# Moving four weight loads ahead of SyncE's wait for the scattered rows

## Chip, cores, metric

The kernel runs on one core of a Trainium2 chip. The metric is the time of one execution in microseconds of device time, as the median of several runs. The engines are named TensorE (PE in the profile, PEld for its weight loads), VectorE (DVE), ScalarE (ACT), GpSimd (POOL) and SyncE (SP). SyncE, ScalarE and GpSimd each have a queue on which they issue DMAs. All these DMAs are carried out by the core's 16 DMA engines.

## What is computed

One layer of a mixer with attention, spatial gating and a recurrence, then a mixture of experts over 512 tokens of width 1024. Only the second part matters here (16 experts of width 512, two for each token):

```python
def hierarchical_moe(x, wg, bg, we, be, w_gate, w_up, w_down):
    ...
    expert_id = g_idx[:, None] * EXPERTS_PER_GROUP + top_i
    combine = jnp.sum(jax.nn.one_hot(expert_id, N_EXPERTS, dtype=jnp.float32)
                      * (g_w * top_p)[..., None], axis=1).astype(x.dtype)
    y = jnp.zeros_like(xt)
    for e in range(N_EXPERTS):
        h = jax.nn.silu(xt @ w_gate[e]) * (xt @ w_up[e])
        y = y + combine[:, e:e + 1] * (h @ w_down[e])
    return y.reshape(b, s, d)
```

## The kernel before

The kernel doesn't run every expert over every token. It computes the router's choice for four blocks of 128 tokens (t = 0 to 3), gives each token and each of its two experts a place (`slot_idx`), and scatters the normalised rows `xn2` into the DRAM tensor `slots`, grouped by expert and padded to tiles of 128 rows. `scatter(t)` on GpSimd (line 640) issues two indirect DMAs for each block of tokens, so eight in all, 512 KB each; each raises the semaphore `scattered` by 16. Then the experts' tiles run one after the other. A tile is 128 rows of one expert.

Each matmul in f32 is made of three, with operands split in a high and a low part. So each 512 KB block of weights that lands is first copied to `w_hi` by ScalarE (L371, L378), then VectorE subtracts it to give `w_lo` (L383, L389), then TensorE uses both (`expert_block`, L1352; its matmuls are L1052 to L1054). `w_hi` and `w_lo` have four slots, so a split waits until TensorE has used the block four before it.

A tile has twelve blocks: r = 0 to 3 of the gate weights, r = 4 to 7 of the up weights, and r = 8 to 11 of the down weights. **The down blocks that stand in a tile belong to the tile before it**, because a tile's hidden values are ready only when its gate and up products are. The blocks land alternately in two sets of twelve buffers, `EVEN` and `ODD` (lines 307 to 311), each with a semaphore of its own (`even_in`, `odd_in`). The second tile uses `ODD`; its r = 8 to 11 are `raw_mg` buffers 3 to 6 and hold the down weights of expert 0.

A tile's rows are read from `slots` by SyncE (`load_rows`, L503), into `x_odd` or `x_even`, then turned by eight transposes on TensorE (`turn_x`, L1342), copied as high part by ScalarE (L922) and as low part by VectorE (L1958). The first tile is an exception: its rows are gathered by matmuls (`place0`, L1295), not read. So the first rows that go through `slots` are those of the second tile, and TensorE turns them between blocks 5 and 6 of the first tile (L1372, L1373). Later tiles' rows are turned ahead of block 8 of the tile before. The results of a tile are stored back to `slots` by ScalarE (L943, and L1028 for the one before the last) and gathered by GpSimd at the end (L656).

SyncE works through its program in order; whatever stands behind a wait of its own is issued later. Around the change its program is: first tile's gate and up blocks (`EVEN`, L492), second tile's gate and up blocks (`ODD`, L498; its last three, into `raw_mg`, wait until TensorE is done with the output projection's weights), then the wait for all eight scatters (L525), the read of the second tile's rows (L526), the four down blocks (L528), the read of the third tile's rows (L530), then the third tile's blocks. `load_rows` also waits for the semaphore `xT_ps`, which TensorE raises in the first tile behind its block 0 (L1371). Each of the loads is one DMA of 512 KB.

Of the kernel before, what the change touches and what calls it, by code (L numbers as in the profile page):

```python
# [32 lines left out]
NT = TOK // P  # L33
# [61 lines left out]
PER_EXPERT = TOK // P  # L95
# [18 lines left out]
def build(nc, a, out):  # L114
# [10 lines left out]
    with ctx:  # L125
        def sem(name):
            return ctx.enter_context(nc.semaphore(name))
# [146 lines left out]
        def y_hi(t):  # L274
# [6 lines left out]
        S = {n: sem(n) for n in (  # L281
            "g1_spread ones_done x0_sq_done x0_stat x0_rstd x0_norm x0_turned xn_hi_done xn_done "
            "hi_act lo_pool lo_dve w_used taken "
            "ident_done consts_pool consts_dve zero_done zeros_stored "
            "g1_in chan_in diag_in sgu_in relb_in toep_filled toep_out bias_in bias_done route_in g2_in "
            "sgu_raw sguT_ps sguT_done mask_done sv_sq sv_stat sv_rstd sv_done sp_exp chan_done "
            "conv_done gates_ps gates_done "
            "decay_done mult_in mult_done u_done c_mid b_mid ch bh c_ready b_ready mix_ps "
            "scores_ps biased exped normed probsT_ps probsT_done out_ps a_hi a_ready "
# [40 lines left out]
        x_even, x_odd, y_even, y_odd = (xn2[:, n, :] for n in range(4))  # L330
# [77 lines left out]
        def _(sp):  # L408
# [10 lines left out]
            def load_block(places, r, src):  # L419
                bufs, sems = places  # L420
                sp.dma_start(bufs[r].rearrange("p (k n) -> p k n", k=2), src).then_inc(sems[r], 16)

            def tile_source(e, before, r):

                if r < 4:
                    return rows2(w_g[e], 2 * r, 0)
                if r < 8:
                    return rows2(w_u[e], 2 * (r - 4), 0)
                return rows2(w_d[before], 2 * (r % 2), 512 * ((r - 8) // 2))
# [70 lines left out]
            def load_rows(block, dst, landed_in, turned):  # L500

                sp.wait_ge(S["xT_ps"], turned)
                sp.dma_start(dst, slots[bass.ds(block * P, P), :]).then_inc(landed_in, 16)  # L503
# [18 lines left out]


            sp.sem_inc(S["x_even_in"], 16)
            sp.wait_ge(S["scattered"], 16 * 2 * NT)  # L525
            load_rows(PER_EXPERT, x_odd, S["x_odd_in"], 1)  # L526
            for r in range(8, PER_TILE):
                load_block(ODD, r, tile_source(1, 0, r))  # L528
                sp.sem_inc(even_in[r], 16)
            load_rows(2 * PER_EXPERT, x_even, S["x_even_in"], 1)  # L530
            for r in range(PER_TILE):
                if r == 8:
# [40 lines left out]
        def _(pool):  # L573
# [43 lines left out]
            for r, (base, pattern) in enumerate((  # L617
                    (0, [[PER_EXPERT * P, NE]]), (P, [[0, NE], [P, PER_EXPERT - 1]]),
                    (NE * PER_EXPERT - 1, [[-PER_EXPERT, NE], [-1, PER_EXPERT - 1]]),
                    (NE, [[-1, NE], [0, PER_EXPERT - 1]]), (0, [[1, NE]]), (0, [[PER_EXPERT, NE]]),  # L620
                    (1, [[PER_EXPERT, NE], [1, PER_EXPERT - 1]]))):
                n = 1
                for _, c in pattern:
                    n *= c
                pool.iota(route[:, 19 + r, 0:n], pattern=pattern, base=base, channel_multiplier=0,
                          allow_small_or_imprecise_dtypes=True)\
                    .then_inc(S["consts_pool"], 1)
# [421 lines left out]
        def _(pe):  # L1049
# [73 lines left out]
            def key_pieces(jp, which):  # L1123

                for (h0, *a), (h1, *b) in zip(together(jp, which)[0::2], together(jp, which)[1::2]):
                    w = a[-1]
                    piece = 2 * P if w > 2 * P else P
                    for k0 in range(0, w, piece):
                        for h, (g, i, at, _) in ((h0, a), (h1, b)):
                            yield h, g, i, at, k0, min(w, k0 + piece)  # L1130
# [1005 lines left out]
```

## Time and profile before

| | before |
|---|---|
| median of 3 runs | 788.7 us (787.71 to 789.83) |
| the profiled execution | 789.02 us |
| its span in the profile | 787.3 us |
| mean granted TensorE clock | 0.996 of full speed |
| TensorE busy | 764.9 us, 97% |
| VectorE / ScalarE / GpSimd busy | 63% / 57% / 27% of the span |
| moved by DMA | 206.74 MB, of it on SyncE's queue 188.80 MB |

The span is the time between the first and the last instruction that the profiler recorded; the device time is a little longer. All positions below are microseconds from the start of the span. The expert tiles run from about 470 us to about 765 us. A matmul's busy time is pipelined: a matmul of 0.39 us begins every 0.23 us, so a busy TensorE is not one at its peak, but a gap between two of them is a true gap. A DMA's "landing" is counted from its issue to the arrival of its last byte. The queue numbers in the DMA rows: q1 is SyncE's, q10 ScalarE's, q0 GpSimd's.

### The profile page before, as it was taken

Reading aid. Unit: us, or ns where it says so; the run is one execution under the profiler, and the core shown is the slowest. Engines: PE = TensorE matmul, PEld = TensorE weight load, DVE = VectorE, ACT = ScalarE, POOL = GpSimd, SP = SyncE. Lnnn points to the kernel's source line nnn. Section 1 sums busy time; section 2 is a strip of 40 time slices with the busy share of each in tenths; the row PEclk is TensorE's granted clock in tenths of the full one; section 3 lists DMA queues with packets and bytes.
Section 4 is the critical chain, followed back from the end, with each engine's and each line's share of the span. In section 5 each row is a group of like instructions: output and inputs, shape, how many; then the busy total and the mean of one; then the engine's idle time right before and its main releaser. Section 6 shows DMA issues by size and latency. Waiting matters only on the chain.

```text
span 787.3 us, 10839 instructions
## 1 busy us (share of the span) xinstructions
PE 764.9 (97%) x3739; PEld 621.8 (79%) x3739; DVE 492.3 (63%) x702; ACT 450.5 (57%) x590; POOL 209.3 (27%) x124
## 2 busy tenths in 40 slices
PE   7999999999999999999999999999999999999994
PEld 4788777777787888888888788878778888888782
DVE  5704476585743302322022669999999998999888
ACT  5244657566744232323321556787878888888862
POOL 3644433232332444434442532000000000000033
PEclk9999999999999999999999999999999999999998
DMA  8569999792222262332328438999999999999965
GB/s 300 183 213 381 370 337 393 268 342 75 69 66 81 81 214 87 100 107 81 107 97 282 161 131 285 408 409 409 409 409 409 410 409 410 409 409 341 398 251 202
DMA packets 134318, 206.74 MB, mean 263 GB/s; under 512 B 10813, under 2 KB 65669, under 8 KB 134278
## 3 DMA queue, kind: packets, MB, share of 16 engines
q1 hardware_dynamic: 126084, 188.80, 65.7%
q10 hardware_dynamic: 5890, 9.04, 3.1%
q0 software_dynamic: 2304, 8.39, 2.8%
q8 instruction: 24, 0.39, 0.2%
q14 instruction: 16, 0.13, 0.0%
HBM read 157.95 MB, written 48.25 MB: 262 GB/s over the span
## 4 chain that ended last, share of the span: by engine, by line
PE 85%; DVE 6%; ACTq 2%; DMA 2%; POOL 2%; ACT 1%; issue 1%; DVEq 0%; SPq 0%; POOLq 0%
PE ps L1052 25%; PE ps L1054 24%; PE ps L1053 24%; DVE w_lo L389 3%; PE ps L1342 2%; PE ps L1146 1%; PE ps L1174 1%; PE ps L1157 1%; PE ps L1295 1%; POOL raw_mg L656 1%; PE ps L1269 1%; DMA x<-in_x 1%; PE ps L1349 1%; ACTq L877 1%; DMA raw_mg<-slots,slot_idx 1%
## 5 line engine op out<-in xcount | busy, mean ns | idle before, releaser
L383 POOL TENSOR_TENSOR w_lo<-raw,w_hi 128x1024 fp32r<-128x1024 f32 x72 | 174.1, 2422 | 250.4 <-ACT w_hi L371 250.4
L371 ACT ACTIVATE w_hi<-raw 128x1024 fp32r<-128x1024 f32 x73 | 76.8, 1057 | 195.4 <-PE ps L1054 168.0
L1052 PE MATMUL ps<-xn_hi,w_hi 128*128 128x512 f32 x352 | 140.6, 399 | 0.0
L1054 PE MATMUL ps<-xn_hi,w_lo 128*128 128x512 f32 x352 | 137.2, 390 | 0.0
L1053 PE MATMUL ps<-xn_lo,w_hi 128*128 128x512 f32 x352 | 137.1, 390 | 0.0
L1052 PE MATMUL ps<-w_hi,xT_hi 128*128 128x512 f32 (+1 forms) x248 | 97.0, 391 | 2.2 <-DVE w_lo L389 2.2
L1054 PE MATMUL ps<-w_hi,xT_lo 128*128 128x512 f32 (+1 forms) x248 | 95.1, 384 | 0.0
L1053 PE MATMUL ps<-w_lo,xT_hi 128*128 128x512 f32 (+1 forms) x248 | 94.9, 383 | 0.0
L656 POOL DMA_INDIRECT raw_mg<-slots,slot_idx x7 | 7.8, 1113 | 280.4 <-DMA slots<-y_tile 278.5
L1052 PEld LDWEIGHTS ps<-xn_hi,w_hi 128*128 128x128 f32 x352 | 66.1, 188 | 16.2 <-issue 2.0
L1053 PEld LDWEIGHTS ps<-xn_lo,w_hi 128*128 128x128 f32 x352 | 66.1, 188 | 14.1 <-issue 1.0
L1054 PEld LDWEIGHTS ps<-xn_hi,w_lo 128*128 128x128 f32 x352 | 66.1, 188 | 14.0
L1715 DVE SCALAR_TENSOR_TENSOR macc<-raw,ps 128x512 f32<-128x512 f32 x16 | 11.0, 688 | 94.0 <-PE ps L1054 93.8
L389 DVE TENSOR_TENSOR w_lo<-raw_mg,w_hi 128x1024 fp32r<-128x1024 f32 x57 | 67.7, 1221 | 1.1 <-ACT w_hi L378 0.7
L378 ACT ACTIVATE w_hi<-raw_mg 128x1024 fp32r<-128x1024 f32 x57 | 59.2, 1055 | 8.3 <-PE ps L1054 8.3
L1052 PEld LDWEIGHTS ps<-w_hi,xT_hi 128*128 128x128 f32 x248 | 46.6, 188 | 12.8 <-DVE w_lo L389 4.3
L389 DVE TENSOR_TENSOR w_lo<-raw,w_hi 128x1024 fp32r<-128x1024 f32 x43 | 51.3, 1220 | 5.9 <-ACT w_hi L378 5.8
L1054 PEld LDWEIGHTS ps<-w_hi,xT_lo 128*128 128x128 f32 x248 | 46.6, 188 | 9.2
L378 ACT ACTIVATE w_hi<-raw 128x1024 fp32r<-128x1024 f32 x43 | 44.9, 1056 | 14.8 <-PE ps L1054 10.9
L1053 PEld LDWEIGHTS ps<-w_lo,xT_hi 128*128 128x128 f32 x248 | 46.7, 188 | 8.4
L1052 PE MATMUL ps<-w_hi,hT_hi 128*128 128x512 f32 x128 | 51.2, 400 | 0.6 <-DVE hT_lo L1965 0.6
L1053 PE MATMUL ps<-w_lo,hT_hi 128*128 128x512 f32 x128 | 49.9, 390 | 0.0
(311 smaller groups left out, 1475.1 us busy)
## 6 DMA issues: line engine op xcount, KB each, us to landing
slots<-raw SPq DMA_DIRECT2D x65, 512.0 KB, 7.0
raw<-in_w_in SPq DMA_DIRECT2D x52, 512.0 KB, 4.0
raw_mg<-in_exp_w_down SPq DMA_DIRECT2D x35, 512.0 KB, 11.0
raw<-in_exp_w_gate SPq DMA_DIRECT2D x29, 512.0 KB, 11.3
raw_a<-in_exp_w_gate SPq DMA_DIRECT2D x26, 512.0 KB, 10.6
raw_c<-in_exp_w_up SPq DMA_DIRECT2D x24, 512.0 KB, 11.8
raw_mg<-in_exp_w_up SPq DMA_DIRECT2D x22, 512.0 KB, 11.9
raw<-in_exp_w_up SPq DMA_DIRECT2D x15, 512.0 KB, 11.8
```

The lines of the kernel that those rows point to most:

```text
L371: nc.scalar.activation(w_hi[:, b % HI_SLOTS, :], raw_buf(b), ACT.Copy)\
L378: nc.scalar.activation(w_hi[:, (8 + r) % HI_SLOTS, :], buf, ACT.Copy).then_inc(S["hi_act"], 1)
L383: eng.tensor_tensor(w_lo[:, b % HI_SLOTS, :], raw_buf(b), w_hi[:, b % HI_SLOTS, :].bitcast(F32), ALU.subtract)\
L389: nc.vector.tensor_tensor(w_lo[:, (8 + r) % HI_SLOTS, :], place(at, r)[0], w_hi[:, (8 + r) % HI_SLOTS, :].bitcast(F32), ALU.subtract)\
L656: pool.indirect_dma_start(dst, None, slots, bass.IndirectOffsetOnAxis(ap=slot_idx[:, 2 * t + k:2 * t + k + 1], axis=0))\
L877: act.dma_start(router_w[:, :, NG:], a["router_exp_w"][0].rearrange("(k p) n -> p k n", p=P))\
L1052: pe.matmul(dst, hi_l, hi_r, start=start, stop=False)
L1053: pe.matmul(dst, hi_l, lo_r, start=False, stop=False)
L1054: return pe.matmul(dst, lo_l, hi_r, start=False, stop=stop)
L1146: mm = pe.matmul(score_home(g, h)[:, home + k0:home + k1], qT[rows, jp % 2, i * P:(i + 1) * P], kT[rows, jp % 2, k0:k1], start=True, stop= ...
L1342: mm = pe.transpose(ps[:, 3 + k // 4, (k % 4) * P:(k % 4 + 1) * P], rows[:, k * P:(k + 1) * P], ident[:, :])
L1715: dve.scalar_tensor_tensor(out=macc[:, 1, :], in0=gate_buf[:, g % 3, :], scalar=1.0, in1=ps[:, 2 + c, :], op0=ALU.add, op1=ALU.mult)\
```

## The change

On SyncE, the loop that issues the four down blocks of the second tile (r = 8 to 11 of `ODD`) moves from behind the read of that tile's rows to ahead of the wait for the scatters, so that it stands directly behind the tile's up blocks. Each pass also raises `even_in[r]` by 16, which goes with it. The loads, their sources and their destinations are the same, and no wait is added or removed.

```diff
@@ -522,11 +522,11 @@
             sp.sem_inc(S["x_even_in"], 16)
-            sp.wait_ge(S["scattered"], 16 * 2 * NT)
-            load_rows(PER_EXPERT, x_odd, S["x_odd_in"], 1)
             for r in range(8, PER_TILE):
                 load_block(ODD, r, tile_source(1, 0, r))
                 sp.sem_inc(even_in[r], 16)
+            sp.wait_ge(S["scattered"], 16 * 2 * NT)
+            load_rows(PER_EXPERT, x_odd, S["x_odd_in"], 1)
             load_rows(2 * PER_EXPERT, x_even, S["x_even_in"], 1)
             for r in range(PER_TILE):
                 if r == 8:
```

## Rows read from the trace of the kernel before

**Rows 1.** The page of the profile: busy us (share of the span) and instructions by engine.

```profile
PE 764.9 (97%) x3739; PEld 621.8 (79%) x3739; DVE 492.3 (63%) x702; ACT 450.5 (57%) x590; POOL 209.3 (27%) x124
```

**Rows 2.** Waits from 486 us to the end: total us, times, longest.

```profile
ACT w_hi L378 <- PE ps L1054: 41.4, 84, 1.4
...
PEld ps L1052 <- DVE w_lo L389: 4.3, 5, 1.3
...
DVE raw_mg L2060 <- DMA raw_mg<-slots,slot_idx: 0.6, 1, 0.6
```

**Rows 3.** Stretches: us, busy PE, PEld, DVE, ACT, POOL; PEclk, DMA share, GB/s.

```profile
470.70:477.00 6.30, 6.28 (x56) 5.80 (x55) 4.64 (x22) 2.80 (x4) 2.82 (x4) 1.00 1.02 358
477.00:483.00 6.00, 6.00 (x39) 5.18 (x38) 5.34 (x10) 4.54 (x8) 2.28 (x2) 1.00 0.59 240
483.00:484.00 1.00, 1.00 (x6) 0.84 (x5) 1.00 (x2) 0.71 (x2) 0.00 (x0) 1.00 0.06 8
...
600.00:700.00 100.00, 100.00 (x475) 83.23 (x474) 91.35 (x86) 84.20 (x92) 0.00 (x0) 1.00 1.05 409
```

**Rows 4.** SyncE's issues in order of time: start us, us, line, what, count.

```profile
469.32 1.41 SPq L421 DMA_DIRECT2D raw_mg<-in_exp_w_up  x2
...
483.00 0.34 SPq L503 DMA_DIRECT2D xn<-slots  x1
483.38 2.03 SPq L421 DMA_DIRECT2D raw_mg<-in_exp_w_down  x4
```

**Rows 5.** Waits of SyncE's queue, 455 to 492 us; columns as rows 2.

```profile
SPq L502 <- PEq L1371: 7.8, 1, 7.8
SPq L503 <- DMA slots<-xn,slot_idx: 4.4, 1, 4.4
```

**Rows 6.** DMA issues at 483.00, 484.9 and 485.51; last: us to landing.

```profile
xn<-slots SPq DMA_DIRECT2D x1, 512.0 KB, 3.3
...
raw_mg<-in_exp_w_down SPq DMA_DIRECT2D x1, 512.0 KB, 8.7
...
xn<-slots SPq DMA_DIRECT2D x1, 512.0 KB, 9.4
```

**Rows 7.** TensorE's weight loads, then ScalarE, by time; [idle us, releaser].

```profile
487.08 1.02 PEld L1342 LDWEIGHTS ps<-ident,xn 128*128 128x128 f32 x8
...
490.85 0.19 PEld L1052 LDWEIGHTS ps<-w_hi,first_hi 128*128 128x128 f32 x1 [0.20 <-DVE first_lo L1958]
...
502.14 0.14 PEld L1342 LDWEIGHTS ps<-ident,xn 128*128 128x128 f32 x1
...
498.55 1.06 ACT L378 ACTIVATE w_hi<-raw_mg 128x1024 fp32r<-128x1024 f32 x1 [0.29 <-PE ps L1054]
```

**Rows 8.** Two of GpSimd's scatters: start us, us.

```profile
472.17 1.03 POOL L646 DMA_INDIRECT slots<-xn,slot_idx  x1 [0.89 <-DVE slot_idx L1826]
...
478.20 1.38 POOL L646 DMA_INDIRECT slots<-xn,slot_idx  x1 [0.30 <-issue]
```

**Rows 9.** Landing: scatters 466-468, 472-474, 476-479; L943's 13 stores; L1028's.

```profile
DMA to landing us min/median/max: 3.4/3.6/3.9
...
DMA to landing us min/median/max: 5.6/5.7/5.7
...
DMA to landing us min/median/max: 4.8/4.9/5.0
...
DMA to landing us min/median/max: 5.9/6.1/6.9
...
slots<-y_tile ACTq DMA_DIRECT2D x1, 512.0 KB, 2.6
```

**Rows 10.** DMA queues, 470.7 to 475 and 514.5 to 515: packets, MB.

```profile
q1 hardware_dynamic: 712, 1.39, 100.3%
...
q10 hardware_dynamic: 33, 0.14, 65.6%
q1 hardware_dynamic: 38, 0.07, 37.1%
```

## The prediction

> **What bounds the kernel now.** I read the page first. TensorE is busy 97% of the 787.3 us span [rows 1]. So an edit of the loads can only matter where TensorE waits for something that a load brings, or where it is made to wait. I then listed the waits from 486 us to the end, that is all expert tiles: ScalarE's longest total is for TensorE (84 times), TensorE waits for VectorE's low halves (5 times, 4.3 us at the weight loads), and the one wait of the three for a DMA is VectorE's 0.6 us for a gather at the end [rows 2]. The stretch from 600 to 700 us says the same: TensorE is busy 100 of 100 us while the DMA engines run full at 409 GB/s [rows 3]. Weights are there in time, although their engines have no air.
>
> Then SyncE's issues in order of time [rows 4]. The last up block of the second tile is issued at about 470.7 us (469.32 + 1.41 us). Then SyncE sits for 12.3 us: its waits name TensorE's release of the first turn (7.8 us) and the scattered rows (4.4 us) [rows 5]. At 483.00 it issues the row read of the second tile (x_odd), at 483.38 to 485.41 the four down blocks that the change moves [rows 4], then the next row read and the third tile's blocks.
>
> Are these down blocks late? The last of them lands 8.7 us after its issue at 484.9 [rows 6], at 493.6, and the others before it. ScalarE splits the first at 498.55, because TensorE releases a slot of w_hi then, and TensorE comes to the tile's turn, which stands ahead of them, at 502.14 [rows 7]. All four have landed 5 us before the first is split. The same goes for what is issued behind them: the third tile's rows land at 494.9 (485.51 + 9.4) for a turn at 502.14 [rows 6, 7]. **Earlier landing of all of these is worth nothing.**
>
> The tight transfer is another one, the row read at 483.00. It takes 3.3 us [rows 6], so the rows are there at 486.3, and TensorE's turn of them starts at 487.08 directly behind the matmul before it [rows 7]. The slack is **0.8 us**. The turn is in TensorE's own order, so later rows stop it. Behind it hang ScalarE's and VectorE's first_hi and first_lo, for which TensorE waits 0.20 us even now at 490.85 [rows 7]. A delay of the rows beyond 0.8 us goes whole into the span.
>
> **The change, part by part.**
>
> *Four issues of SyncE move up.* They cost 2.03 us of SyncE [rows 4] and move from behind the wait to 470.7 to about 473, into time in which SyncE sat for 12.3 us: nothing on the path. The wait that they are moved past doesn't hold anybody else back: behind it on SyncE stand the row reads and the third tile's blocks, as now. The next row read and those blocks come up to 2.0 us nearer behind the wait: with 7 us of slack, also nothing.
>
> *Four loads of 512 KB move into the time of the scatters.* That has a price. The eight scatters run on GpSimd's queue; the first of the last four is issued at 472.17 and the last at 478.20 [rows 8]. The last lands at 483.0, 4.8 us behind its issue [rows 9], and this is what SyncE waits for. From 470.7 to 477 the DMA engines are full now; from 477 to 483 they are 59% busy and from 483 to 484 6% [rows 3]. The moved blocks are 2.10 MB, 5.1 us at 409 GB/s. The air up to 484 is 0.41 x 6 + 0.94 x 1 = 3.4 us. So 1.7 us doesn't fit, and the rest fits only beside the last two scatters.
>
> What does SyncE's traffic do to a scatter? The trace shows it three times.
> (a) The pair of scatters issued between 466 and 468, before the up blocks, lands in 3.4 and 3.9 us; the pair issued between 472 and 474, when the three up blocks are under way, in 5.6 and 5.7 [rows 9]. The difference of the means is 5.65 - 3.65 = 2.0 us.
> (b) ScalarE's stores of 512 KB take 6.1 us (median of 13) beside SyncE's stream, and 2.6 us in the one case at 754.67 when the loads are over [rows 9]: 3.5 us more. Between 514.5 and 515 such a store gets 33 packets to SyncE's 38, with 0.14 MB to 0.07 MB [rows 10]; so engines take turns packet by packet, and the larger packets of the store (and of a scatter) get two thirds.
> (c) The last two scatters themselves, when nothing of SyncE is in flight, take 5.0 and 4.8 us [rows 9].
>
> The moved traffic is still there when the last scatter runs. By 475 SyncE's queue has moved 1.39 of the up blocks' 1.57 MB [rows 10], so the down blocks begin at about 475.5; with a third of 0.41 MB a us beside the scatters some 0.6 of their 2.10 MB are moved by 480. So the last scatter meets what (a) and (b) show. Its delay is bounded by 0.9 us (its landing becomes the 5.7 of (a)) and 3.5 us (the whole of (b)). I take 2.0 us, (a)'s difference, since it is the same instruction on the same queue.
>
> *The row read.* It is issued at about 485.0. From 475.5 to then the engines can move 9.5 x 0.41 = 3.9 MB, of which the four scatters take 2.1 MB, so 1.8 MB of the down blocks are through and 0.3 MB, 0.7 us, stand ahead of the read. The 1 us that the read takes to its first packet anyhow hides them (issued at 483.00, the engines 6% busy until 484 [rows 3]). So I keep 3.3 us, with 0 to 1 us more as the bound. The rows land at 485.0 + 3.3 = 488.3, against 487.1 needed.
>
> The sum: 2.0 us (scatter) + 0 (read) - 0.8 us (slack) = **1.2 us** of new TensorE stall ahead of the first turn, everything behind it shifted. The bounds are 0.9 - 0.8 = 0.1 us and 3.5 + 1.0 - 0.8 = 3.7 us. It isn't given back later: VectorE's short stalls of TensorE come from its extra work inside single tiles, and with four slots of w_hi it can't run ahead by more than four blocks.
>
> The Trainium skill (DMA: Bandwidth & Descriptors, Rules for kernel authors) says to issue a DMA early and wait late, so that its fixed cost is hidden. Here the measured slack of 5 us and more says that it is hidden already; by that rule alone the sum would be a gain or zero, never a loss. The same page gives about 358 GB/s as what HBM yields to one core; the trace has 409 over 100 us [rows 3]. By the page's figure the moved blocks would take an estimated 5.9 us, and 2.5 us instead of 1.7 us would not fit.
>
> **The rivals.**
>
> *No stall.* The last scatter is held up by less than 0.8 us: its packets are twice as large as SyncE's, and the moved blocks sink into the 3.4 us of air. For it speaks (c): the pair was slow even alone, so its 4.8 us may be the time of its own queue and not of the wire. Against it: (a) and (b), both over 2 us. Time: 788.7.
>
> *Slower by more than can be overlooked.* Place: the same turn. The scatters wait behind the stream like ScalarE's stores, +3.5 us, and the third and fourth of them queue behind each other; the read then finds a rest of the down blocks ahead of it, +0.5 us. 3.5 + 0.5 - 0.8 = 3.2 us: 791.9. It decides from the point at which the last scatter lands later than 486.2 (483.0 + 0.8 + 2.4), where the stall passes 2.4 us. For it: in the changed kernel SyncE's stream is as dense during all four scatters as it is beside the stores. Against it: the first pair, in a full stream too, paid only 2.0 us.
>
> *A gain.* The whole load stream runs ahead by up to 5.1 us, which needs a consumer that waits for a load. The waits show none in the tiles [rows 2]; the 0.2 us at 490.85 is VectorE's, and if all of it went the time would be 788.5. To be seen as a gain it would need 2.4 us, and I find nowhere that it could come from.
>
> *The change doesn't do what it says*: that the down blocks still go late, because a full queue stopped SyncE. Two of the up blocks' issues together take 1.41 us [rows 4] and SyncE then sits idle, so it is not likely. 788.7.
>
> **How the numbers follow.** The profiled run took 789.0 us with a span of 787.3 us, so 1.7 us lie around the span; the median of the three runs is 788.7 us, 0.3 us less than the profiled one. The stall adds to either: span 788.5, profiled run 790.2, median 788.7 + 1.2 = 789.9.
> Chances: forecast (stall of 0.3 to 2.3 us) 0.60; no stall, the undone change with it, 0.22; the slower rival 0.15; a gain 0.03. About 0.3%, 2.4 us, is what a measurement of this kernel can tell from no change. Faster by more: 0.03. Slower by more: 0.15 from the rival. Same: 0.82. The range runs from the no-stall case, less 0.6 us because the three runs before lie 1 us to either side, 788.1, to the slower rival's 791.9. What is left out are its upper part and the gain.
>
> **What would show it.** Right: in the profile of the changed kernel four issues into raw_mg<-in_exp_w_down stand at 470.7 to 473; DMA share is near 1 from 477 to 483; the last scatter lands in 6 to 7.5 us; the row read is issued at 484.5 to 486; and TensorE shows a gap of 1 us or so ahead of the first eight L1342 transposes, then the same pace as now. Wrong on size: a read at 486.2 or later. Wrong altogether: a read at 483 to 483.8 and no gap, or waits in later tiles that get shorter, which would mean that some load was late after all.

## The result

| | before | after |
|---|---|---|
| median | 788.65 us (787.71 to 789.83, 6 runs) | 793.61 us (793.18 to 795.77, 6 runs) |
| ratio | | 1.0068, 95% interval 1.0057 to 1.0079 |
| the profiled execution | 789.02 us | 793.18 us |
| its span | 787.3 us | 791.4 us |
| mean granted TensorE clock | 0.996 | 0.993 |

The change makes the kernel 5.0 us slower, by more than the 0.3% that can be told from no change. I had forecast 789.9 us, within a range of 788.1 to 791.9.

**The profile after.** SyncE's issues in order of time (start, us, what, count), and under them what its queue waited for (total us, times, longest), to be held against [rows 4, 5]:

```profile
467.60 1.80 SPq L421 DMA_DIRECT2D raw_mg<-in_exp_w_up  x3
469.51 2.29 SPq L421 DMA_DIRECT2D raw_mg<-in_exp_w_down  x4
486.27 0.81 SPq L503 DMA_DIRECT2D xn<-slots  x2
487.13 1.87 SPq L421 DMA_DIRECT2D raw_a<-in_exp_w_gate  x3
...
SPq L503 <- DMA slots<-xn,slot_idx: 8.9, 1, 8.9
SPq L502 <- PEq L1371: 5.4, 1, 5.4
```

The four down blocks stand at 469.51, right behind the three last up blocks. The row read moved from 483.00 to 486.27, and the wait for the scattered rows grew from 4.4 to 8.9 us. The head of the kernel, up to the up blocks, is 1.3 us shorter in this profile (467.60 against 468.91; it lies between 467.60 and 469.30 in the profiles of this study). So I count from the issue of the first of these three up blocks ("from the up blocks"): the read was issued at +14.1 us and is now issued at +18.7 us, 4.6 us later.

The chain that ended last says what the read waited for (start, us, what), and the weight loads of TensorE what waited for the read (in brackets: idle us before, and what ended it), to be held against [rows 7]:

```profile
476.59 0.30 issue
476.90 9.36 DMA slots<-xn,slot_idx
...
486.27 3.57 DMA xn<-slots
...
489.89 1.76 PE ps L1342 x8
...
485.54 0.19 PEld L1054 LDWEIGHTS ps<-w_hi,xT_lo 128*128 128x128 f32 x1
489.88 1.36 PEld L1342 LDWEIGHTS ps<-ident,xn 128*128 128x128 f32 x8 [4.16 <-DMA xn<-slots]
...
494.96 0.19 PEld L1052 LDWEIGHTS ps<-w_hi,first_hi 128*128 128x128 f32 x1
...
506.32 1.02 PEld L1342 LDWEIGHTS ps<-ident,xn 128*128 128x128 f32 x8
```

The last scatter takes 9.4 us where it took 4.8 [rows 9]. The read itself takes 3.6 us, about its old 3.3 [rows 6]. TensorE's first turn starts at +22.3 us from the up blocks instead of +18.2, with 4.16 us of idle before it. That is 4.1 us lost. But the second turn, which was at 502.14 [rows 7], +33.2 us, is at +38.7: 5.5 us lost. The other 1.4 us is in the stretches behind the gap. The columns are those of [rows 3], the third figure from the end is the granted clock:

```profile
488.00:489.00 1.00, 0.00 (x0) 0.00 (x0) 0.18 (x1) 0.00 (x0) 0.00 (x0) 1.00 0.91 340
...
490.00:491.00 1.00, 1.00 (x6) 1.00 (x7) 0.00 (x0) 0.00 (x0) 0.00 (x0) 0.57 0.82 295
491.00:492.00 1.00, 1.00 (x6) 0.90 (x5) 0.00 (x0) 0.31 (x1) 0.00 (x0) 0.50 0.97 336
492.00:493.00 1.00, 1.00 (x4) 0.81 (x3) 0.26 (x1) 0.71 (x1) 0.00 (x0) 0.50 0.91 295
493.00:494.00 1.00, 1.00 (x4) 0.77 (x4) 1.00 (x2) 0.00 (x0) 0.00 (x0) 0.72 0.98 346
494.00:495.00 1.00, 1.00 (x6) 0.79 (x5) 1.00 (x1) 0.94 (x1) 0.00 (x0) 1.00 0.96 367
```

The clock was 1.00 in all of this stretch before. Behind the gap it is 0.50, which is 1.2 GHz of 2.4 GHz, for 3.4 us. From the second turn on the two kernels run at the same pace (the turns before the last tile's end are 5.5 us apart, as the second ones are), so nothing is given back. 5.5 us less the 1.3 us of the shorter head is 4.2 us, about the 4.1 us between the spans.

### The profile page after: what moved, and what is told of

Read it like the earlier page. It is cut to its first block, busy times and chain, and to the rows that moved or that the text cites. A ratio compares the mean times of both kernels' runs of the same rounds, so it can differ in the third digit from the quotient of the medians.

```text
span 791.4 us, 10839 instructions
## 1 busy us (share of the span) xinstructions
PE 765.3 (97%) x3739; PEld 622.2 (79%) x3739; DVE 495.4 (63%) x702; ACT 450.5 (57%) x590; POOL 208.8 (26%) x124
## 4 chain that ended last, share of the span: by engine, by line
PE 83%; DVE 6%; DMA 3%; ACTq 2%; POOL 2%; ACT 1%; issue 1%; DVEq 0%; POOLq 0%
PE ps L1052 25%; PE ps L1054 24%; PE ps L1053 24%; DVE w_lo L389 3%; PE ps L1342 2%; PE ps L1146 1%; PE ps L1174 1%; PE ps L1157 1%; DMA slots<-xn,slot_idx 1%; POOL raw_mg L656 1%; PE ps L1269 1%; ACTq L877 1%; PE ps L1349 1%; DMA raw_mg<-slots,slot_idx 1%; DVE xT_lo L1958 1%
## 5 line engine op out<-in xcount | busy, mean ns | idle before, releaser
L1053 PEld LDWEIGHTS ps<-xn_lo,w_hi 128*128 128x128 f32 x352 | 66.1, 188 | 14.1 <-issue 1.0
L1054 PEld LDWEIGHTS ps<-xn_hi,w_lo 128*128 128x128 f32 x352 | 66.1, 188 | 14.1
```

The source lines that it names most:

```text
L1053: pe.matmul(dst, hi_l, lo_r, start=False, stop=False)
L1054: return pe.matmul(dst, lo_l, hi_r, start=False, stop=stop)
```

## The experiments

All start from one of the two kernels. The table gathers what I read for each of them in the same way: the time as a ratio to the kernel before, run on the same chip; then, in us from the up blocks, when the row read was issued (that is, when the last scatter had landed, or what held it); the idle time before TensorE's first turn; the loss at that turn and at the second turn against the kernel before. The ratio is of medians of several executions, while the other columns come from one profiled execution each.

| kernel | ratio (95% interval) | read issued | gap | loss at 1st turn | at 2nd turn |
|---|---|---|---|---|---|
| before | | +14.1 | none | | |
| e_few_bytes | 1.0000 (0.9990 to 1.0010) | +14.8 | none | 0.0 | 0.0 |
| e_one_early | 1.0007 (0.9997 to 1.0017) | +15.4 | 0.5 | 0.5 | 0.3 |
| e_two_early | 1.0037 (1.0025 to 1.0049) | +17.3 | 2.4 | 2.4 | 2.2 |
| e_three_early | 1.0062 (1.0045 to 1.0078) | +18.3 | 3.5 | 3.5 | 4.6 |
| after (four) | 1.0068 (1.0057 to 1.0079) | +18.7 | 4.2 | 4.1 | 5.5 |
| e_rows_free | 1.0000 (0.9988 to 1.0013) | none | none | 0.0 | 0.0 |
| e_read_held5 | 1.0051 (1.0034 to 1.0068) | +17.3 | 2.6 | 2.5 | 3.9 |
| e_read_held | 1.0069 (1.0047 to 1.0091) | +18.6 | 3.7 | 3.7 | 5.0 |
| e_wide_rows | 1.0088 (1.0071 to 1.0104) | +19.1 | 4.7 | 4.7 | 6.0 |
| e_after_third_pair | 1.0061 (1.0044 to 1.0078) | +18.3 | 4.1 | 4.1 | 6.6 |
| e_ups_landed | 1.0091 (1.0074 to 1.0108) | +19.1 | 4.9 | 4.8 | 7.0 |
| e_after_fourth_pair | 1.0077 (1.0060 to 1.0094) | +19.1 | 4.9 | 4.8 | 6.1 |

One row needs care: the profiled execution of `e_after_third_pair` took 795.90 us at a mean clock of 0.991, its three others 793.44 to 793.68 us at 0.993. So its 6.6 us don't belong to its ratio, which stands for some 4.8 us.

### Is it the scatter, the read and the turn? e_rows_free, e_read_held

`e_rows_free` keeps the four blocks early and the scatters as slow as in the changed kernel, but the first turn no longer needs them (it turns rows of the input `x`, one more early read of 512 KB):

```diff
+            sp.wait_ge(S["w_used"], B_EXP)
+            sp.dma_start(raw_mg[:, 7, :], a["x"][0, 0:P, :]).then_inc(S["x_odd_in"], 16)
             for r in range(8, PER_TILE):
                 load_block(ODD, r, tile_source(1, 0, r))
                 sp.sem_inc(even_in[r], 16)
             sp.wait_ge(S["scattered"], 16 * 2 * NT)
-            load_rows(PER_EXPERT, x_odd, S["x_odd_in"], 1)
...
-                    turn_x(x_odd, S["x_odd_in"], 16)
+                    turn_x(raw_mg[:, 7, :], S["x_odd_in"], 16)
```

> All four down blocks stay early, but the second tile's rows are no longer taken from the scattered ones: 128 rows of the input x are read instead, into another buffer and ahead of the down blocks, so that the first turn waits for no scatter. This leaves out the true rows of the second tile. The scatters are as slow as in the changed kernel or slower (9 us for the last). Theory: no gap ahead of the first turn, no fall of the clock, time of the kernel before within 0.5 us, 788.2 to 789.2. Rival (early traffic costs in another way, by contention for memory, by late weights or by its place on SyncE): 792 to 794.

Its third tile's row read (the first that needs the scatters), and TensorE's first turn, in order of time:

```profile
486.61 0.34 SPq L503 DMA_DIRECT2D xn<-slots  x1
...
486.08 0.19 PEld L1055 LDWEIGHTS ps<-w_hi,xT_lo 128*128 128x128 f32 x1
486.31 1.02 PEld L1343 LDWEIGHTS ps<-ident,raw_mg 128*128 128x128 f32 x8
```

The scatters are through at 486.61, +18.5 us from its up blocks (468.15), as late as in the changed kernel. The turn follows the matmul before it without a gap, at +18.2 as in the kernel before, and the time is that of before: 1.0000. So the whole loss goes through this one dependency. A late weight or other contention could cost no more than the interval leaves, 1.0 us, and the trace shows 0.0 us at both turns.

`e_read_held` moves no block. It holds the row read until TensorE has used block 5 of the first tile (`e_read_held5`, further down, until block 4):

```diff
             sp.wait_ge(S["scattered"], 16 * 2 * NT)
+            sp.wait_ge(S["w_used"], B_EXP + 6)
             load_rows(PER_EXPERT, x_odd, S["x_odd_in"], 1)
```

> The order of the kernel before, but SyncE waits ahead of the row read until TensorE has used block 5 of the first tile (w_used at least B_EXP + 6, about 487.0 in the trace of before). No block moves. The rows land 3.3 us later, about 490.4, against 487.1 needed: a gap of 3.3 us with scatters that are as fast as before. It measures the price of the gap alone. Theory: the gap itself and TensorE's clock behind it, 3.3 + about 1.3 us, so before + 4.6 us, clock near 0.5 for about 3 us behind the gap. Rival (the fall of the clock comes from the denser DMA traffic, not from the gap): before + 3.3 us and clock 1.00 throughout.

```profile
490.71 1.35 PEld L1343 LDWEIGHTS ps<-ident,xn 128*128 128x128 f32 x7 [3.72 <-DMA xn<-slots]
...
490.00:491.00 1.00, 0.28 (x2) 0.28 (x3) 0.00 (x0) 0.00 (x0) 0.00 (x0) 0.84 0.92 258
491.00:492.00 1.00, 1.00 (x6) 1.00 (x6) 0.00 (x0) 0.00 (x0) 0.00 (x0) 0.50 0.84 190
...
493.00:494.00 1.00, 1.00 (x4) 0.81 (x3) 0.22 (x1) 0.75 (x1) 0.00 (x0) 0.50 1.01 352
```

A gap of 3.7 us, the clock at 0.50 behind it, 5.0 us lost at the second turn, ratio 1.0069: it nearly reproduces the changed kernel's loss (5.5 us) with scatters that are as fast as before and no moved traffic. The rival for the clock (denser traffic) falls, from the other side too: `e_rows_free` has the denser traffic and no gap, and its clock was 1.00 there.

### How much traffic? e_one_early, e_two_early, e_three_early, e_few_bytes

The first n of the four blocks ahead of the wait, the others behind the read (here n = 1):

```diff
-            for r in range(8, PER_TILE):
+            for r in range(8, 9):
                 load_block(ODD, r, tile_source(1, 0, r))
                 sp.sem_inc(even_in[r], 16)
             sp.wait_ge(S["scattered"], 16 * 2 * NT)
             load_rows(PER_EXPERT, x_odd, S["x_odd_in"], 1)
+            for r in range(9, PER_TILE):
+                load_block(ODD, r, tile_source(1, 0, r))
+                sp.sem_inc(even_in[r], 16)
```

> Only the first of the four down blocks is issued ahead of the wait for the scatters, the other three stay behind the row read. Theory (the moved blocks hold up the scatters, the scatters the row read, the read TensorE's first turn): the changed kernel's last scatter landed 486.3 - 481.7 = 4.6 us later than before once the two traces are laid over each other (its head is 1.3 us shorter), 1.15 us for each of the four blocks. One block: the last scatter lands in about 6 us instead of 4.8, 1.15 - 0.8 us of slack = 0.4 us of stall, time of before + 0.4 us. Rival (the idle 3.4 us of the DMA engines take up the first blocks, only the overhang counts): last scatter 4.8 to 5.0 us, no stall, time of before. Rival (it is the issue or the order on SyncE, not the bytes): no statement on the scatter; a quarter of the loss, about 1.2 us.

> Two of the four down blocks ahead of the wait. Theory: last scatter 4.8 + 2.3 = 7.1 us, stall 2.3 - 0.8 = 1.5 us, time of before + 1.5 us, and more only if TensorE's granted clock falls behind the gap as it did behind the 4.2 us gap of the changed kernel (0.50 to 0.57 from 490 to 493). Rival (idle time takes up the first 3.4 us, that is 2.7 blocks): no stall, time of before.

> Three of the four down blocks ahead of the wait. So far the last scatter landed 14.1 us behind the issue of the first of the three up blocks with none moved (before), 15.4 with one, 17.3 with two, 18.7 with four. Theory (once SyncE's queue has work throughout, the four scatters get a fixed share and more blocks change nothing): 18.3 to 18.8 us, gap of 3.7 to 4.1 us, time as with four, before + 4.5 to 5.5 us. Rival (each block adds its own time): 18.0 us between two and four, gap 3.3 us, before + 3.5 us, if TensorE's clock doesn't fall.

TensorE's first turn in the runs with one, two and three blocks (start, us; in brackets idle before and its releaser), then the granted clock of two stretches behind it with two blocks:

```profile
487.49 0.85 PEld L1345 LDWEIGHTS ps<-ident,xn 128*128 128x128 f32 x8 [0.53 <-DMA xn<-slots]
...
489.24 0.86 PEld L1345 LDWEIGHTS ps<-ident,xn 128*128 128x128 f32 x8 [2.42 <-DMA xn<-slots]
...
490.42 1.57 PEld L1345 LDWEIGHTS ps<-ident,xn 128*128 128x128 f32 x8 [3.48 <-DMA xn<-slots]
...
490.00:491.00 1.00, 1.00 (x8) 0.86 (x6) 0.00 (x0) 0.63 (x1) 0.00 (x0) 1.00 0.84 236
491.00:492.00 1.00, 1.00 (x6) 0.81 (x5) 0.57 (x1) 0.57 (x2) 0.00 (x0) 1.00 1.02 342
```

One block costs 1.3 us of the scatters' time, two cost 3.2 us, three 4.2, four 4.6. The idle time of the DMA engines doesn't take up the first 2.7 blocks: that rival falls with the first block. Nor is it one price for each block: my 2.3 us for two was 0.9 us short, and from three on it hardly grows. For three I had left open 18.3 to 18.8 (saturation) or 18.0 (proportion); 18.3 leans to saturation, and together with the 18.7 of four it fits it.

`e_few_bytes` keeps four early issues at the same place, with an eighth of the bytes, and issues the true blocks behind the read:

```diff
             for r in range(8, PER_TILE):
-                load_block(ODD, r, tile_source(1, 0, r))
-                sp.sem_inc(even_in[r], 16)
+                sp.dma_start(odd_buf[r].rearrange("p (k n) -> p k n", k=2)[:, :, 0:64],
+                             tile_source(1, 0, r)[:, :, 0:64]).then_inc(S["small"], 16)
             sp.wait_ge(S["scattered"], 16 * 2 * NT)
             load_rows(PER_EXPERT, x_odd, S["x_odd_in"], 1)
+            sp.wait_ge(S["small"], 64)
+            for r in range(8, PER_TILE):
+                load_block(ODD, r, tile_source(1, 0, r))
+                sp.sem_inc(even_in[r], 16)
```

> Four DMAs are issued early at the same place and into the same four buffers, but each carries only an eighth (64 of 512 columns, 64 KB, rows of 256 bytes); the full down blocks are issued behind the row read as before, so 1.6 us more of SyncE behind the read. Theory (bytes on the shared DMA engines hold up the scatters): 0.26 MB is half a block, though in small packets, last scatter at 14.1 to 15.4 us behind the first up issue, gap 0 to 0.5 us, before + 0 to 0.6 us. Rival (four more issues, or their place on SyncE, cost): as with four full blocks, before + 4 to 5 us.

The read is issued at +14.8, inside the 0.8 us of slack, and the time is that of before. So it is bytes, not issues, and not the number of packets either: the four small DMAs are 1024 packets of 256 bytes, as many as the four whole blocks have of 2 KB.

### What sets the scatters' pace? e_wide_rows, and the queues of the changed kernel

The two queues in three stretches of the changed kernel, one microsecond each (packets, MB, share of 16 engines; q1 is SyncE's, q0 GpSimd's): 475 to 476, 477 to 478, 483 to 484. Under them, from issue to landing, the first and then the two last of the four late scatters (minimum, median, maximum):

```profile
q1 hardware_dynamic: 96, 0.18, 101.6%
...
q0 software_dynamic: 66, 0.27, 65.6%
q1 hardware_dynamic: 73, 0.14, 36.5%
...
q0 software_dynamic: 65, 0.26, 63.7%
q1 hardware_dynamic: 71, 0.14, 34.9%
...
DMA to landing us min/median/max: 8.2/8.2/8.2
...
DMA to landing us min/median/max: 8.9/9.1/9.4
```

The scatter issued at 470.87 has no packet until past 476. Then, for 8 us, the queues take turns packet by packet, 66 to 73 and 65 to 71, and the scatters have 0.26 to 0.27 MB a us. The four scatters' 2.1 MB need 7.8 us at that, from 476.4 to 484.2. A handful of last packets come one by one until 485.7, and the read is issued at 486.27.

If turns are by packet, larger packets on SyncE's queue take more:

```diff
             for r in range(8, PER_TILE):
-                load_block(ODD, r, tile_source(1, 0, r))
+                sp.dma_start(odd_buf[r], w_d[0][(r - 8) * P:(r - 7) * P, :]).then_inc(odd_in[r], 16)
                 sp.sem_inc(even_in[r], 16)
```

> The changed kernel, but each of the four early loads reads 128 whole rows of 4 KB of the down weights instead of 256 half rows of 2 KB: the same bytes in half the packets. The down products of the first expert are wrong by it. Theory (the engines take packets of the two queues in turn, so with 2 KB against 4 KB the scatters had two thirds): now one half, so the four scatters' 2.1 MB need up to 10.3 us instead of 7.8; the last lands 20 to 21.5 us behind the first up issue instead of 18.7, gap 5.5 to 7 us, before + 7 to 9 us. Rival (the share is by bytes, or the scatters' pace is their own): last scatter at 18.3 to 18.9 us, before + 5 us.

The queues from 480 to 481 in this run:

```profile
q1 hardware_dynamic: 61, 0.20, 50.4%
q0 software_dynamic: 60, 0.20, 50.2%
```

60 and 61 packets, 0.20 and 0.20 MB: the share is by packets, as forecast. The last scatter landed at +19.1 and not at 20 to 21.5: I had given SyncE's queue the traffic for all 8 us, but of its blocks much was through before the scatters began, and in the last 2 us these had the engines nearly alone. The Trainium skill (DMA: Bandwidth & Descriptors, Queues, rings and completion order) says that each engine takes turns between the queues it has work for, packet by packet; these stretches agree with it, and they don't show its other figure, some 9 to 17 descriptors to a packet. Nor is it known whether what the profile counts as a packet is the page's.

### Why do the scatters start so late? e_ups_landed, e_after_third_pair, e_after_fourth_pair

In the kernel before, the first packet of the third pair of scatters came 6.0 us from the up blocks, when SyncE's queue had moved 1.37 MB. With any number of whole blocks early, with wide rows too, it came at +7.8 to +8.8 us, and in each of these runs when SyncE's queue had moved 1.87 to 1.97 MB (three up blocks are 1.57 MB). That is nearly the same number of bytes each time, whatever stood behind them. (`e_few_bytes`, with 0.26 MB more queued, lies between: +7.1 us, at 1.59 MB.) It looks as if a newcomer waits until what has been handed to the engines already is through, and as if that were some fixed amount. Three kernels issue the down blocks later, behind a wait of SyncE's:

```diff
+            sp.wait_ge(odd_in[7], 16)
             for r in range(8, PER_TILE):
                 load_block(ODD, r, tile_source(1, 0, r))
```

In the two others the wait is for a new semaphore that GpSimd raises behind each scatter that it issues (`S["small"]` at least 6, or 8).

> The changed kernel, but SyncE waits ahead of the four down blocks until the last up block has landed, 7.7 us behind the first up issue, so that they don't queue behind it. Theory: the first pair of the last four scatters lands as before (5.6 and 5.7 us), the second pair meets the down blocks at full strength: 4.8 becomes 7 to 8 us, last scatter at 16.5 to 17.5 us behind the first up issue, and the row read then waits for the rest of the down blocks ahead of it on SyncE's queue, 4.5 to 5.5 us instead of 3.3: gap 3.5 to 5 us, before + 4 to 6 us. Rival (only the depth of SyncE's queue at the moment at which a scatter is issued counts, and it is shallow here): last scatter at 15 us, before + 1 us.

> The changed kernel, but SyncE issues the four down blocks only when GpSimd has issued the third of its four pairs of scatters, 5.7 us behind the first up issue instead of 1.9. In the runs with two, three and four blocks early the first packet of the third pair came 8.4 to 9.0 us behind the first up issue, in the kernel before 6.1. Theory (that slip of 2.6 us is of blocks queued ahead of the pair): first packet at 6.1 us, the third pair lands near its 5.6 and 5.7 us, at most 7; the last pair meets the stream, last scatter at 16 to 17.5 us, gap 2.5 to 4 us, before + 3 to 5.5 us. Rival (the slip comes whenever the stream starts or runs): as the changed kernel or worse, as in the run that waited for the up blocks, last scatter at 18.5 to 19.5 us.

> As the run before, but the down blocks wait until all eight scatters are issued, about 10.7 us behind the first up issue. Theory: their packets come behind those of the last scatter, which lands at 14.1 to 15 us; now the row read stands behind 2.1 MB on SyncE's own queue and takes 5 to 6.5 us instead of 3.3: gap 1.5 to 3 us, before + 1.5 to 4.5 us. So the hold-up moves from the scatter to the read. Rival (the read doesn't wait for blocks ahead of it): read 3.3 to 3.8 us, gap below 1 us, before + 0 to 1 us.

SyncE's issues in the first and the last of the three, and the queues of the last from 476 to 477 and from 479 to 480:

```profile
476.80 2.55 SPq L421 DMA_DIRECT2D raw_mg<-in_exp_w_down  x4
487.56 0.82 SPq L503 DMA_DIRECT2D xn<-slots  x2
...
476.39 3.22 SPq L421 DMA_DIRECT2D raw_mg<-in_exp_w_down  x4
487.29 0.81 SPq L503 DMA_DIRECT2D xn<-slots  x2
...
q0 software_dynamic: 113, 0.40, 97.3%
...
q1 hardware_dynamic: 38, 0.08, 53.5%
```

GpSimd raised the semaphore ahead of the work of the scatter that it should have followed: the blocks went out at 471.85, between the two scatters of the third pair (471.49 and 472.82), and at 476.39, ahead of the last scatter (477.49). So `e_after_third_pair` didn't test what it was to test; its blocks were queued when the pair's packets were due, and its first packet came at +7.7, when SyncE's queue had moved 1.82 MB. The other two did free the third pair: in the last run it has the engines for itself from 476 to 477. But the last pair paid for it. Its scatters were issued at 476.02 and 477.49, with nothing of SyncE's in flight and the rest of the third pair ahead of them, and their packets began past 480, more than 4 us after the first of the two issues, while SyncE's own packets crawled: 38 of them in a microsecond, 0.08 MB, where some 200 of 2 KB go in the steady stream (409 GB/s, [rows 3]). The last scatter landed at +19.1. Both my estimates (+16.5 to 17.5, and +14.1 to 15) and the rival of the queue's depth at the time of issue are refuted. Wherever the four blocks are issued between +1.9 and +8.4 us, the last scatter comes at +18.3 to +19.1. That a newcomer waits behind a fixed amount is consistent with the runs in which SyncE's stream was running already, and is not shown for the runs in which it starts beside a scatter. Why the engines crawl there stays open. Packets from half rows of the down weights are slow in the changed kernel also (96 in the microsecond from 475, at a full share) and move more bytes in `e_wide_rows` (0.34 MB in the microsecond from +7), but no run separates that from the rest.

### What does the gap itself cost? e_read_held5

> As the kernel before, but the row read waits until TensorE has used block 4 of the first tile (w_used at least B_EXP + 5), one block of 1.36 us earlier than in the run that held it until block 5. Gap 3.7 - 1.4 = 2.3 us. Theory (the clock fell behind the gap of 3.7 us and of 4.2 us, not behind the 2.4 us of the run with two blocks): clock 1.00 throughout, time before + 2.2 to 2.5 us. Rival (any gap of over 1 us brings a fall): before + 4 us, clock near 0.5 for 3 us.

```profile
488.59 1.26 PEld L1343 LDWEIGHTS ps<-ident,xn 128*128 128x128 f32 x8 [2.56 <-DMA xn<-slots]
...
489.00:490.00 1.00, 1.00 (x8) 1.00 (x6) 0.00 (x0) 0.00 (x0) 0.00 (x0) 0.50 0.80 199
...
491.00:492.00 1.00, 1.00 (x4) 0.81 (x3) 0.66 (x1) 0.31 (x1) 0.00 (x0) 0.50 1.02 365
```

I was wrong here: 2.6 us of gap brought the fall, 0.50 for 3.4 us, where the 2.4 us of `e_two_early` had not in the profiled execution. Even that isn't a firm edge. Of the nine executions of `e_two_early` eight took 790.53 to 791.71 us with a mean clock of 0.995 to 0.997, and one took 793.91 us with 0.993, the value of the kernels whose clock fell; it has no trace, but it looks as if the clock fell there too.

The clock's price is the difference of the two losses in the table: 1.1 to 1.4 us where it fell for 3.4 us (after, three early, both held reads, wide rows, fourth pair), 2.2 and 2.5 us in `e_ups_landed` and `e_after_third_pair`, where it stayed at 0.50 for 6.8 us. The stretch at 0.50 doesn't always start behind the gap. Here are a microsecond of `e_three_early` and one of `e_ups_landed`, in which TensorE did nothing and the clock was falling or down:

```profile
489.00:490.00 1.00, 0.00 (x0) 0.00 (x0) 0.39 (x1) 0.00 (x0) 0.00 (x0) 0.94 1.04 340
...
490.00:491.00 1.00, 0.00 (x0) 0.00 (x0) 0.00 (x0) 0.00 (x0) 0.00 (x0) 0.50 0.85 336
```

In the changed kernel and `e_read_held5` all of the stretch lies behind the gap, and it costs 1.4 us. In `e_three_early` it starts at 489.9, half a microsecond before TensorE's turn at 490.42, and costs 1.1 us. In `e_ups_landed` it starts at 489.9, 1.6 us before the turn, and its 6.8 us cost 2.2 us. So the part that falls into the gap has nothing to slow down. Nor does the length go with the kernel: of the four executions of `e_after_third_pair` the profiled one alone had the mean clock of 0.991 that goes with 6.8 us, and one of the four of `e_read_held` had it as well (795.82 us, the others 793.26 to 794.03). Where it didn't fall, 0.2 us came back: TensorE's wait for first_lo, 0.20 us before [rows 7], was gone.

## Why the prediction was wrong

**Held.** TensorE is the bound and no load in the tiles is waited for; the moved blocks had slack and earlier landing brings nothing (`e_rows_free`: 1.0000). The tight transfer is the row read. The scatters are held up by SyncE's traffic, in part by turns of packets with two thirds for the scatters. The read keeps its time (3.6 us against 3.3). A delay beyond 0.8 us goes whole into the span and, but for 0.2 us, isn't given back. The direction, slower, and the place are as forecast; the last scatter's landing fits the condition of the slower rival, 486.2 in the time of the trace before: it landed at +18.7, which is 487.6 there.

**The step that failed is the size of the scatter's delay.** I took 2.0 us, from the pair that had met the up blocks, and 3.5 us as the upper bound, from ScalarE's stores. It was 4.6 us: 2.8 us because the first packet of the four scatters came later (+8.8 against +6.0 us), and 1.8 us because they then took longer, 9.8 us from there to the last landing against 8.0. Two things went into it that I had looked at and not used.

- The pair of [rows 9] was no measure for a full stream. SyncE's queue ran dry a microsecond behind that pair's first packet, so it had the engines nearly for itself, and it began after only 1.37 MB of SyncE's traffic. With more blocks behind, its first packets slipped by 1.8 to 2.8 us.
- The four scatters form a queue of their own. In the trace before, the first pair was nearly through when the second came. At two thirds of the engines the four take 7.8 us, longer than the 6.0 us between the first and the last issue [rows 8], so the first pair's late start moves the last scatter as well. I added a delay to a single scatter, where a start time and a rate for four were wanted: 477.7 (the first packet, in the time of the trace before) + 7.8 + 2 (the last few packets and the report) = 487.5, against 487.6 measured. The 7.8 us could have been had from [rows 10]; the start and the 2 us are read from the changed kernel, so this describes the result and doesn't foretell it. Why the start slips stays open.

An upper bound from the nearest row (3.5 us) was no bound, since the row was of a single store in a stream and not of four scatters one behind the other.

**A missing term: TensorE's clock.** I priced the gap at its own length. The clock at half speed behind it added 1.4 us. With it the slower rival, 3.2 us of stall, would have read 4.6 us, and the range would have ended at 793.3 us, close to the 793.6 measured. The forecast's own stall, 1.2 us, lies between the gaps of 0.5 and 2.4 us whose profiles show no fall.

**The chances.** 0.15 for slower was too little. The arguments for "no stall" (larger packets, idle engines, the last pair's own slowness) are all refuted by `e_one_early`, where a single block used up the slack. The rule that I had weighed there, to issue a DMA early and wait late (the Trainium skill, DMA: Bandwidth & Descriptors, Rules for kernel authors), would have given a gain or zero. It speaks of the fixed cost alone; for a load that has slack already and shares the engines with one that hasn't, the early issue cost 5.0 us. Both rows that I held against "no stall", (a) and (b), stood above the slack of 0.8 us, so the slower case should have had far more weight than 0.15.

The sum with what was measured: 4.6 us (last scatter) + 0.3 us (read) - 0.8 us (slack) = 4.1 us of stall, + 1.4 us of clock = 5.5 us at the second turn; the medians differ by 5.0 us, the difference being within what the heads of single runs vary by.

No version came out faster than the kernel before. With the rows free of the scatters the time is that of before, so the old order loses nothing at this place that these runs could show.

## What to carry to other kernels

A load that isn't late gains nothing by going early, and it can hold up a small transfer on another queue that somebody waits for: look at which transfer has the least slack, and ask what shares the engines with it. Price such a delay for the whole queue of transfers ahead of the awaited one, as a start time plus bytes at the shared rate, not as a surcharge on the last one. And price a gap of TensorE with the clock behind it: in the profiled executions with a gap of 2.6 us or more it cost 1.1 to 2.5 us more.

## What I had not expected of the hardware

- Two queues with packets waiting take turns about one for one, so the share of bytes follows the size of the packets: 0.27 to 0.14 MB a us with 4 KB against 2 KB, 0.20 to 0.20 with 4 KB on both.
- A transfer on one queue doesn't start beside a running stream at once. Its first packets came when the stream had moved on by about 0.5 MB more than before, at 1.87 to 1.97 MB in six kernels that had at least one whole block more queued. How many blocks stood behind made no difference to that; a quarter of a megabyte more queued moved it less (1.59 MB).
- A microsecond can pass with the engines half busy and a fifth of the usual bytes (0.08 MB from 479 to 480 in `e_after_fourth_pair`, against 0.41). The cause is open.
- TensorE's granted clock fell to 0.50 in or behind gaps of 2.6 us and more, and not behind the 2.4 us that was profiled; one of nine executions of that kernel looks as if it fell there too. It stayed at 0.50 for 3.4 us in six profiles and 6.8 us in two, with gaps of 4.1 and 4.9 us, and by their mean clocks executions of one and the same kernel differ in this. The length of the gap doesn't tell which.
